# Rotating queries and keys inside the RWKV scan, and starting a projection inside its normalisation, in a two-layer hybrid block on one core

## The reference

```python
def _modulate(x, shift, scale):
    return _ln_plain(x) * (1.0 + scale) + shift

def _apply_rope(x, cos, sin):
    xr = x.reshape(sh[:-1] + (2, 2, DH_A // 4))
    x1, x2 = xr[..., 0, :], xr[..., 1, :]
    return jnp.stack([x1 * c - x2 * s, x2 * c + x1 * s], axis=-2).reshape(sh)

def _latent_diff_attn(q, k, v, kc, vc, cos, sin, lam):
    qr = _apply_rope(q, cos, sin)
    kr = _apply_rope(k, cos, sin)
    ...
        return _diff_attend([(q_rot, kr, v), (q_plain, kc, vc)], lam)
```

## Time and profile before

| | us |
|---|---|
| median of 3 runs (lowest, highest) | 4220.05 (4210.33, 4223.99) |
| the profiled execution | 4215.09 |
| its span | 4213.3 |
| TensorE busy | 3603.2 (86%) |
| VectorE, GpSimd, ScalarE busy | 1541.4, 1049.8, 987.9 (37, 25, 23%) |
| mean granted clock | 0.935 |

### The profile page before, as it was taken

One profiled execution on the slowest core, in us unless ns is written; L12 is line 12 of the kernel. 1 busy time (PEld: TensorE's weight loads), 2 busy tenths in 40 slices (PEclk: granted clock), 3 DMA queues, 4 the chain that ended last, 5 costly groups with the idle time before them and its releaser, 6 DMA issues. The chain is left out here.

```text
span 4213.3 us, 80793 instructions
## 1 busy us (share of the span) xinstructions
PE 3603.2 (86%) x36124; PEld 2680.1 (64%) x36124; DVE 1541.4 (37%) x2258; ACT 987.9 (23%) x1763; POOL 1049.8 (25%) x641
## 2 busy tenths in 40 slices
PE   4979999998887777899899497999997877669987
PEld 3658888886556553788744275888776554438843
DVE  2234333431775244221101524444552763241102
ACT  2322121221554120222100141222221442213300
POOL 1122222222334111322100222222232432224401
PEclk8989999999998889899999798999998989889998
DMA  5653333322004240222243144333332112413331
GB/s 199 211 172 99 103 106 104 102 79 75 35 35 142 71 137 22 65 64 63 75 165 130 36 155 134 92 95 112 103 113 71 51 64 98 160 30 97 93 100 40
DMA packets 432706, 410.71 MB, mean 97 GB/s; under 512 B 14244, under 2 KB 367706, under 8 KB 425450
## 3 DMA queue, kind: packets, MB, share of 16 engines
q1 hardware_dynamic: 430778, 396.77, 30.0%
q10 hardware_dynamic: 1584, 8.78, 0.5%
HBM read 325.15 MB, written 80.35 MB: 96 GB/s over the span
## 5 line engine op out<-in xcount | busy, mean ns | idle before, releaser
L799 PE MATMUL ps<-I-280_h_hi,I-1976_w_hi 128*128 128x256 f32 (+1 forms) x832 | 300.2, 361 | 25.0 <-POOL I-1977_w_lo L393 15.0
L799 PE MATMUL ps<-I-280_h_hi,I-1977_w_lo 128*128 128x256 f32 (+1 forms) x832 | 283.9, 341 | 0.4 <-issue 0.4
L799 PE MATMUL ps<-I-281_h_lo,I-1976_w_hi 128*128 128x256 f32 (+1 forms) x832 | 283.9, 341 | 0.0
L2042 PE MATMUL ps<-I-21315_w_down,I-18155_hf 128*128 128x512 f32 x528 | 234.0, 600 | 9.0 <-DMA I-21315_w_down<-in_ffn_down 9.0
L799 PE MATMUL ps<-I-22064_h_hi,I-23479_w_hi 128*128 128x512 f32 (+1 forms) x544 | 216.3, 398 | 20.9 <-POOL I-23480_w_lo L393 15.8
L799 PE MATMUL ps<-I-22065_h_lo,I-23479_w_hi 128*128 128x512 f32 (+1 forms) x544 | 202.7, 373 | 0.4 <-issue 0.4
L799 PE MATMUL ps<-I-22064_h_hi,I-23480_w_lo 128*128 128x512 f32 (+1 forms) x544 | 202.5, 372 | 0.0
L402 PE MATMUL ps<-I-18156_h_hi,I-18365_w_hi 128*128 128x512 f32 x704 | 180.3, 337 | 15.7 <-POOL I-18366_w_lo L393 15.7
L778 POOL CAST I-1976_w_hi<-I-1975_w_raw 128x1024 fp32r<-128x1024 f32 x52 | 56.1, 1079 | 548.9 <-PE ps L799 534.6
L2042 PEld LDWEIGHTS ps<-I-21315_w_down,I-18155_hf 128*128 128x128 f32 x528 | 99.2, 191 | 143.1 <-issue 133.2
L799 PEld LDWEIGHTS ps<-I-280_h_hi,I-1976_w_hi 128*128 128x128 f32 x832 | 158.2, 190 | 42.6 <-POOL I-1977_w_lo L393 15.7
(11 more groups left out here) (838 smaller groups left out, 8322.6 us busy)
## 6 DMA issues: line engine op xcount, KB each, us to landing
I-1975_w_raw<-in_w_in SPq DMA_DIRECT2D x52, 512.0 KB, 5.7
I-23478_w_raw<-in_w_in SPq DMA_DIRECT2D x52, 512.0 KB, 5.0
I-21319_ada_w<-in_ada_w SPq DMA_DIRECT2D x24, 1024.0 KB, 5.0
I-18364_w_raw<-in_ffn_up SPq DMA_DIRECT2D x44, 512.0 KB, 3.9
I-37219_w_raw<-in_ffn_up SPq DMA_DIRECT2D x44, 512.0 KB, 3.9
proj_d<-I-1978_result SPq DMA_DIRECT2D x52, 384.0 KB, 2.8
I-502_ada_w<-in_ada_w SPq DMA_DIRECT2D x16, 1024.0 KB, 5.8
I-21315_w_down<-in_ffn_down SPq DMA_DIRECT2D x22, 512.0 KB, 5.9
```

The lines of the kernel that those rows point to most:

```text
L799: m = pe.matmul(bank(6 + i % 2, n_c), w[:, k, :], hv[:, k, c0:c0 + n_c], start=k == 0 and v == 0, stop=k == KT - 1 and v == 2)
L2042: m = pe.matmul(bank(t), hf[:, g * KG + k, t * P:(t + 1) * P], ring[:, i % SL, k, :], start=g == 0 and k == 0, stop=g == NG - 1 and k == K ...
```

## The change

Two edits that don't depend on one another.

**Normalisation.** `norm` has no block of its own any more: it is called inside the block of `rwkv_inputs` or `ffn`, so its work and that of the projection stand one behind the other on each engine without a meeting in between. The weights of product 0 are loaded at the start, `split_hi(0)` stands on ScalarE ahead of the square root, `split_lo(0)` on GpSimd ahead of the roundings. Product 0's k step j waits for `h_lo` of tile j. Every third `xn` tile is made by ScalarE from a bias computed by a further small VectorE instruction (`neg_mean`); the transposes go through three pairs of PSUM banks instead of four.

**Rotation.** In the scan, once a q or k slot is stored, SyncE fetches its latent part back (one transfer of 128x512, 256 KB) and a second time with the halves exchanged (eight transfers of 16 partitions, 32 KB each); GpSimd does its three operations on them behind a later slot's weight split; SyncE stores the result to `rot_d`. Since `turn_in` and `turn_swapped` are single buffers, a fetch waits until the rotated slot before it has landed. The raw weight ring has two buffers instead of three, and a slot's load is issued one slot later. Attention loads `q_rot` and `k_rot` (and plain q, k, v) and has neither rope table, shuffle nor rotation.

```diff
+        def norm(sc, block, sem, l, i_shift, i_scale, nt, h, xn, hf, rings):
...
+            by_dve = [t for t in range(nt) if t % 3 != 2]
+            by_act = [t for t in range(nt) if t % 3 == 2]
...
+                dve.wait_ge(sem("n_rstd"), 1)
+                dve.scalar_tensor_tensor(nb[:, 0:nt], mv[:, 0:nt, 0], -1.0, rs[:, 0:nt], ALU.mult, ALU.mult).then_inc(sem("n_nb"), 1)
+                for t in by_dve:
+                    dve.tensor_scalar(xn[:, t, :], x[:, t, :], mv[:, t, 0:1], rs[:, t:t + 1],
+                                      ALU.subtract, ALU.mult).then_inc(sem("n_xn"), 1)
+                for j in range(KT):
+                    dve.wait_ge(sem("n_hi"), j + 1)
+                    dve.tensor_tensor(h[1][:, j, 0:n_tok], hf[:, j % 3, 0:n_tok], h[0][:, j, 0:n_tok].bitcast(F32),
+                                      ALU.subtract).then_inc(sem("n_lo"), 1)
+
...
+            def _(pe):
+                pe.wait_ge(sem("n_xn"), len(by_dve))
+                pe.wait_ge(sem("n_xa"), len(by_act))
+                for j in range(KT):
+                    if j >= 3:
+                        pe.wait_ge(sem("n_h"), j - 2)
+                    for t in range(nt):
+                        m = pe.transpose(bank(2 + 2 * (j % 3), P, t * P), xn[:, t, j * P:(j + 1) * P], ident[:, :])
+                    m.then_inc(sem("n_T"), 1)
+
+            @block.scalar
+            def _(act):
...
+                act.wait_ge(sem("n_var"), 1)
+                act.activation(rs[:, 0:nt], rs[:, 0:nt], ACT.Sqrt).then_inc(sem("n_std"), 1)
+                act.wait_ge(sem("n_nb"), 1)
+                for t in by_act:
+                    act.activation(xn[:, t, :], x[:, t, :], ACT.Identity, bias=nb[:, t:t + 1], scale=rs[:, t:t + 1]).then_inc(sem("n_xa"), 1)
+                for j in range(KT):
+                    act.wait_ge(sem("n_T"), j + 1)
+                    if j >= 3:
+                        act.wait_ge(sem("n_lo"), j - 2)
+                    for s, (at, n) in enumerate(BOTH if ctx else LAT):
...
+                    m.then_inc(sem("n_h"), 1)
+
+            @block.gpsimd
+            def _(pool):
+                split_lo(pool, sem, rings, 0)
+                for j in range(KT):
+                    pool.wait_ge(sem("n_h"), j + 1)
+                    pool.tensor_copy(h[0][:, j, 0:n_tok], hf[:, j % 3, 0:n_tok]).then_inc(sem("n_hi"), 1)
...
-                kf = sb(s2, "k_raw", [P, CTILES, TOK])
+                kfk = sb(s2, "k_and_kk", [P, 2, CTILES, TOK])
+                kf, kk = kfk[:, 0], kfk[:, 1]
...
+                xn = kfk[:, :, :, :].rearrange("p a t n -> p (a t n)").rearrange("p (t d) -> p t d", t=NT)
+                norm(s2, block, sem, l, 0, 1, NT, h, xn, rv, rings)
...
+                        if n == 1:
+                            pe.wait_ge(sem("n_h"), KT)
                         if n >= 2:
                             pe.wait_ge(sem("shifted"), n - 1)
-                        fm_product(pe, p_of(n), slot(rings, n), h, range(4), KT, seqs(mains[n]))
+                        for k in range(4):
+                            if n == 0:
+                                pe.wait_ge(sem("n_lo"), k + 1)
...
+                        for k in range(4, KT):
+                            if n == 0:
+                                pe.wait_ge(sem("n_lo"), k + 1)
+                            m = fm_product(pe, p_of(n), slot(rings, n), h, (k,), KT, seqs(mains[n]))
+                        m.then_inc(sem("w_used"), 1)
                         beside(2 * n + 1)
...
-                    for n in range(N):
+                    for n in range(1, N):
...
-            rings = weight_rings(s2, 3, 2)
+            rings = weight_rings(s2, 2, 2)
             res = sb(s2, "result", [P, 2, TOK])
+            rope = sb(s2, "rope", [P, 2, SEQ])
+            rr = sb(s2, "turn_in", [P, SEQ])
+            rs = sb(s2, "turn_swapped", [P, SEQ])
...
+            turned = [s for s, (j, _, _) in enumerate(slots) if J_Q <= j < N_PROJ]
+            swap = [(16 * b, 16 * (b ^ 1)) for b in range(8)]
...
                     sp.dma_start(lvm[:, :, :], A["lvmasks"]).then_inc(sem("const"), 16)
                     load(0)
                     inputs(0)
+                    sp.dma_start(rope[:, :, :], A["rope"]).then_inc(sem("rope"), 16)
                     load(1)
-                    load(2)
+                    def fetch(s):
+                        n = turned.index(s)
+                        src = proj_d[slots[s][0]]
+                        sp.wait_ge(sem(f"stored{s % 2}"), 16 * (s // 2 + 1))
+                        if n:
+                            sp.wait_ge(sem("rot_out"), 16 * n)
+                        sp.dma_start(rr[:, :], src[:, 0:SEQ]).then_inc(sem("turn_in"), 16)
+                        for at_p, from_p in swap:
+                            sp.dma_start(rs[at_p:at_p + 16, :], src[from_p:from_p + 16, 0:SEQ]).then_inc(sem("swap_in"), 16)
+
+                    def put_rotated(s):
+                        sp.wait_ge(sem("rot"), turned.index(s) + 1)
+                        sp.dma_start(rot_d[slots[s][0] - J_Q], rr[:, :]).then_inc(sem("rot_out"), 16)
+
                     g_now, n_in = 0, 0
                     for s, (j, _, widths) in enumerate(slots):
-                        if s + 3 < len(slots):
-                            load(s + 3)
+                        if s + 2 < len(slots):
+                            load(s + 2)
                         w = sum(w for _, w in widths)
                         sp.wait_ge(sem("result"), ends[s])
                         sp.dma_start(proj_d[j, :, 0:w], res[:, s % 2, 0:w]).then_inc(sem(f"stored{s % 2}"), 16)
+                        if s - 2 in turned:
+                            put_rotated(s - 2)
+                        if s - 1 in turned:
+                            fetch(s - 1)
...
-                        pool.wait_ge(sem(f"w_in{s % 3}"), 16 * (s // 3 + 1))
-                        pool.tensor_copy(rings[1][:, s % 2, :, :], rings[0][:, s % 3, :, :]).then_inc(sem("w_hi"), 1)
+                        pool.wait_ge(sem(f"w_in{s % 2}"), 16 * (s // 2 + 1))
+                        pool.tensor_copy(rings[1][:, s % 2, :, :], rings[0][:, s % 2, :, :]).then_inc(sem("w_hi"), 1)
                         split_lo(pool, sem, rings, s)
+                    def rotate(s):
+                        n = turned.index(s)
+                        if n == 0:
+                            pool.wait_ge(sem("rope"), 16)
+                        pool.wait_ge(sem("turn_in"), 16 * (n + 1))
+                        pool.tensor_tensor(rr[:, :], rr[:, :], rope[:, 0, :], ALU.mult).then_inc(sem("rcos"), 1)
+                        pool.wait_ge(sem("swap_in"), 16 * len(swap) * (n + 1))
+                        pool.tensor_tensor(rs[:, :], rs[:, :], rope[:, 1, :], ALU.mult).then_inc(sem("rsin"), 1)
+                        pool.wait_ge(sem("rcos"), n + 1)
+                        pool.wait_ge(sem("rsin"), n + 1)
+                        pool.tensor_tensor(rr[:, :], rs[:, :], rr[:, :], ALU.add).then_inc(sem("rot"), 1)
+
                     pool.memset(S[0][:, :], 0.0).then_inc(sem("zero"), 1)
                     split(0)
                     split(1)
                     for s in range(2, len(slots)):
                         pool.wait_ge(sem("piece"), ends[s - 2])
                         split(s)
+                        if s - 3 in turned:
+                            rotate(s - 3)
...
                     def _(sp):
-                        sp.dma_start(rope[:, :, :], A["rope"]).then_inc(sem("rope"), 16)
                         for j in range(HA):
                             if j >= 2:
                                 sp.wait_ge(sem("s1_mm"), (j - 1) * nq)
                                 sp.wait_ge(sem("v_mm"), j - 1)
-                                sp.wait_ge(sem("rot"), 2 * (j - 1))
+                            sp.dma_start(qr[:, j % 2, :], rot_d[j]).then_inc(sem(f"qr_in{j % 2}"), 16)
+                            sp.dma_start(kr[:, j % 2, :], rot_d[HA + j]).then_inc(sem(f"kr_in{j % 2}"), 16)
                             sp.dma_start(qp[:, j % 2, 0:q_tok], proj_d[J_Q + j, :, 0:q_tok]).then_inc(sem(f"q_in{j % 2}"), 16)
                             sp.dma_start(kp[:, j % 2, :], proj_d[J_K + j]).then_inc(sem(f"k_in{j % 2}"), 16)
                             sp.dma_start(vp[:, j % 2, :], proj_d[J_V + j]).then_inc(sem(f"v_in{j % 2}"), 16)
...
-                                pe.wait_ge(sem("rot"), 2 * j + 2)
+                                pe.wait_ge(sem(f"qr_in{j % 2}"), 16 * (j // 2 + 1))
+                                pe.wait_ge(sem(f"kr_in{j % 2}"), 16 * (j // 2 + 1))
...
-                        def rotate(j):
-                            for i in range(2):
-                                n = 2 * j + i
-                                pool.wait_ge(sem(f"{'qk'[i]}_in{j % 2}"), 16 * (j // 2 + 1))
-                                if n >= 2:
-                                    pool.wait_ge(sem("rot"), n - 1)
```

(18 more changed lines are left out.)

116 lines of the change are left out of this document (34 added, 82 removed).

## The result

The changed kernel takes 4184.79 us in the median of 4 runs (4180.12 to 4190.27), the kernel before 4215.19 beside it: a ratio of 0.9926, with a 95% interval of 0.9902 to 0.995. That is 30 us less where 81 were forecast, 4185 where 4139 was.

What follows compares the result with a forecast made beforehand. TensorE was taken to bound the scans; in normalisation and attention it stood idle behind weights and rotation. Terms -65 - 41 + 25 = -81 took the profiled 4215.09 to 4134, the median 5 above: 4139 us, range 4100 to 4195.

Steps and rivals of the forecast that it cites:

- Part 1, normalisation: Four normalisations: product 0 overlaps them, ending 29.5 us after the statistics begin in place of 48.0; minus 65 us (50 to 72).
- Part 2, attention: Attention: no wait for rotation, first scores 6.8 us earlier, seven heads of layer 1 lose the long unit; minus 41 us.
- Part 3, the scan: Both scans: 32 turned slots add SyncE issues, traffic and GpSimd work; plus 25 us (5 to 62).
- The delay: SyncE in the scan: put, landing and nine fetch issues make all that is queued behind 5.9 us late.
- The rival of the dearer issue: SyncE in the scan: small transfers issue so slowly that turned slots become the bound; 4257 us at 1.3 us each, chance 0.08.
- the in-between case: SyncE in the scan: an issue takes near 0.83 us, cost 50 to 70, time 4164 to 4184 us; chance 0.13.
- The inputs: Layer 1's scan, second place: `sg` 5.5 us late, beside the weights' lateness and not on top.
- The ring and layer 0: Scan: one raw buffer less delays loads at group ends, within layer 1's 15 us; layer 0's lead covers nearly all, 4.
- the cycle: Turned slots in the scan: put, fetch, rotation and next put take 10x + 7.7 us for issue x, a bound above 0.6.
- The contention: Scan: GpSimd's rotation work slows VectorE on shared paths, mostly off TensorE's path; 5 us (0 to 25).
- The rule of the Trainium skill: The eight 32 KB transfers: join small transfers; each paid in full, 3 us, would give 4801 us, chance 0.03.

Runs made afterwards that it cites:

- e9: The changed kernel with the load of slot s+3 directly behind the store of slot s, put and fetch still ahead of outputs and inputs; 4175.35 us.
- e1: The kernel before with the normalisation edit alone, scan and attention as they were; 4152.36 us.
- e3: The kernel before with the normalisation edit and two raw weight buffers in place of three, loads one slot later, no rotation in the scan; 4157.86 us.
- e6: The changed kernel with GpSimd's three operations per turned slot on 8 columns in place of 512, all transfers and waits kept; 4180.68 us.
- e4: The changed kernel with the eight exchanging 32 KB transfers replaced by one of 256 KB that does not exchange the halves; 4159.80 us.
- e10: The changed kernel with the s+3 load directly behind the store of s, put and fetch behind the inputs, GpSimd's rotation one split later; 4141.60 us.
- e8: e3 with the load of slot s+3 directly behind the store of slot s; 4152.43 us.
- e11: e10 with the eight exchanging transfers replaced by one of 256 KB that does not exchange the halves; 4137.52 us.

## Why the prediction was wrong

**Sign and signs of the parts right, size wrong.** Faster was forecast and it is faster. Of the three terms, -65, -41 and +25, the first two came to -55 and -34 and the third to +63. The forecast's 81 became 30 mainly by the third. That 4184.79 lies inside the stated 4100 to 4195 is no merit of the forecast's mechanism: the range took in rivals on both sides. Its upper end was also added up wrongly, as savings of 80 and costs of 62 make 4202 and not 4190.

**Part 1, normalisation: mechanism right.** Product 0's end was forecast 29.5 us after the statistics; it is at 30.5. Measured one product later the savings are 17.5, 17.4, 17.1 and 11.9 us, 64 together; 65 was the sum. The last gave 12 and not 15. Some 2 us of that are its last `h_lo`, which is held by `split_lo(1)`, where I had 1; the rest is open. Of the 9 us between 64 and the table's 55, 7 were not lost in the normalisation: each later product of layer 0's `ffn` stage takes 8.48 us in the changed kernel and 8.32 before (last section).

**Part 2, attention: right, a little too large.** The first scores come 6.7 us sooner (forecast 6.8). Seven heads of layer 1 gain about 2.7 us each, 19 and not 25: the unit that lost its 9.43 us is at 6.2 and not 5.3, and its neighbour went from 4.3 to 4.9. I had taken one unit's excess; the head's length was in the trace and would have been the better row, had I asked what a head must take.

**Part 3, the scan: the step that failed.** Where the loss arises was right: at the ends of groups among or behind turned slots. So was one cause, a load behind outputs and inputs. Four things about it were wrong.

- *The delay.* I put 0.4 + 2.3 + 9 x 0.36 = 5.9 us. It is 9.7 at the place shown and 7.1 to 10.6 over all turned slots with a fetch behind a put: the put was waited for 4.9 us, not 2.7, and an exchanging transfer issues in 0.55. The load then took 7.3 us to the split, not 5.0, with the outputs and inputs on their way around it (twelve inputs; I had written nine, which entered no sum). The rival of the dearer issue named the quantity but wanted 1.2 us, and the in-between case (0.83) had the cost of 50 to 70 that came out, by a price that didn't.
- *The inputs.* I had `sg` 5.5 us late beside the weights' lateness and "not on top", so at nothing. The late inputs hold the chain by themselves: at the second place of layer 1 VectorE waits 7.08 us for `sg` and TensorE 5.39 in the chain, with no wait for weights. Over layer 1 the chain's waits behind ScalarE are 14 us of new idle time, nearly as much as the 16 behind `w_lo`; in e9, where the load goes first, they are 21.
- *The clock.* My sum had no term for it. After the stall of 8.70 us TensorE worked for 4 us at the lower level; over the two scans the same matmuls took 6 and 12 us more.
- *The ring and layer 0.* "Layer 0 has longer products and the lead covers nearly all: 4": it lost 23 us against e1, in three places of 7 to 10 us like layer 1's. And the third buffer, which I had inside the 15 us of layer 1, is 16 us there by itself (e3).

Counted from the start of the scan, the first matmul of a slot comes later than in e1, in us:

| | slot | | | | | |
|---|---|---|---|---|---|---|
| layer 0 | 22: -3.4 | 24: 6.3 | 30: 6.2 | 32: 13.2 | 38: 13.2 | 40: 21.4 |
| layer 1 | 21: 3.6 | 23: 16.8 | 29: 17.0 | 33: 31.4 | 37: 31.8 | 43: 43.8 |

The loss comes in three steps of 7 to 14 us in each layer, and nothing grows within a run of turned slots. That excludes the cycle of the dearer-issue rival: there every turned slot would be longer. The contention, 5 us in the sum, is 4 or less (e6). Of the 69 us over e1, taken out singly, the ring is 12 (e3) and the eight issues are 29 (e4, by stages, what they hold back included). The rest (the put's landing, the fetch, the late inputs) was not taken apart, and the parts don't simply add: reordering both queues (e10) takes 44 of the 69 away with all transfers kept. What stays over e8, the same ring without a rotation, is 7 and 12 us, of which 3 and 2 are the wait for attention's loads behind the scan.

The rule of the Trainium skill that I weighed against the trace (DMA: Bandwidth & Descriptors, "Rules for kernel authors": join many small transfers) pointed the right way, as joining gave 25 us in e4. What decides its size here is what waits behind them: the same joining gave 4 or nothing in e11.

## What to carry to other kernels

When work is moved into a stage with an in-order queue, write down for each queue that it touches what stands behind it at the most crowded place, not on the average; then do the same for the engine that consumes it. A late transfer holds whatever its engine has queued behind the instruction that waits for it, and moving the transfer on one queue only changes which of the two holds first: order both sides together. And a stall of TensorE can cost more than its length: behind the one of 8.70 us here it came back at the lower clock.
